# Ten of 32 modulation rows weighted on TensorE, transposed tiles emptied by two engines, first weights in three parts

## The chip, the cores and the metric

The kernel runs on one core of one Trainium2 chip. The metric is device time in microseconds of one execution of the whole program. The core's engines have instruction queues of their own and meet at semaphores: TensorE (PE, with PEld for its weight loads), VectorE (DVE), ScalarE (ACT), GpSimd (POOL) and SyncE (SP), which here mostly issues DMAs.

## The reference, cut to what matters

A transformer block over 512 tokens of width 1024: adaptive normalisation, one wide input projection, gated linear attention and dilated attention, a merge, and a convolutional FFN. The change touches its very beginning, the first modulation and the first projection:

```
mod = silu(c) @ ada_w + ada_b                  # 1024 -> 6*1024; shift1, scale1 are its first two parts
h = rmsnorm(x, norm1_w) * (1 + scale1) + shift1
... = h @ w_in                                 # av, the attention values, comes first in the kernel
```

## The kernel before, in words

Everything is kept with features on the 128 partitions. x is loaded by tokens, normalised per token on ACT, and transposed by PE into eight tiles of 128 features by 512 tokens (KT = 8; `first_tiles` makes tiles 0 to 3 into banks 3 to 6, `normed_tile(k)` tiles 4 to 7 into the same banks, so tile k waits until tile k-4 has been copied out). ACT copies all eight to xn (`normed_out`).

The modulation of a pair of feature tiles j (j = 0 to 3) needs silu(c) times eight row blocks of ada_w, each 128x512. `ada_sums` on DVE adds the weighted rows k = 0 to 7 into row 0, one scalar_tensor_tensor for each. `shift_scale(j)` on PE then sums over the partitions: a `column_sum` per 128 columns, four narrow products (32 columns of weights, one moving column of ones) each, so 16 products per row. PE may also weight a row itself, by using silu(c) in place of the ones: for j = 1 this is done for row 7 (DIRECT). For j = 0 the sums are made in two halves (`first_sums`, 256 columns each), one for feature tile 0 and one for tile 1, each with its own column sums (`first_shift_scale`) and gain (`first_shift_and_gain`). `shift_and_gain(j)` on DVE adds ada_b and makes the gain.

With gain and shift, ACT makes h_hi (`high(k)`) and the full modulated tile (`modulated(k)`), and DVE the low half h_lo (`lower(k)`); for k = 6 and 7 `modulate_late` on DVE makes the full tile. Each product of the kernel is three: high by high, low by high, high by low. Weights are split likewise: ACT writes w_hi from raw, DVE then w_lo (`early_hi`, `early_lo`, `split_hi`, `split_lo`).

The first projection runs k by k while the modulation is still being made. `first_hi(k)` multiplies h_hi by 256 columns of weights (slot 0 of raw), `wide_hi(k)` by 512 columns (slot 1 for k = 0 to 3, then vx_hi and vx_lo, which come from slot 0 anew), into banks 3 to 6, so after tiles 4 to 7 are copied out. `low_tile(k)` does the products with h_lo. PE's order is written by hand: `low_tile(2j-2)`, `shift_scale(j)`, `low_tile(2j-1)`, `quarter_hi(j)` for j = 1 to 3, then `last_lo`. After that come the dense products of all further units (`product`).

raw has two slots of 1 MB. `load(q)` on SP waits until `raw_used` is at least q-1 (L480), that is, until the split of two loads earlier is done. The first two slots are loaded by `load_early(n, part)`. Part 0 holds the rows k = 0 and 1, part 1 the rest. SP's order: ada_w for j = 0, the four early parts, ada_w for j = 1 and 2, load(2) (the second half of the wide weights, at L480), ada_w for j = 3, load(3), the spill of xn, positions and constants. SP issues in this order: a wait holds up all that is behind it. `raw_used` becomes 1 with `early_lo(0, 1)` and 2 with `early_lo(1, 1)`, both right behind the gain of j = 1 on DVE.

`keep_busy` puts transposes of the identity, which nobody reads, between PE's first steps.

Of the kernel before, what the change touches and what calls it, by code (L numbers as in the profile page):

```python
# [163 lines left out]
DIRECT = {1: KT - 1}  # L164
ADA_STEPS = [2 * KT] + [KT - (j in DIRECT) for j in range(1, KT // 2)]
FIRST_SUMS = [(0, range(0, 4)), (1, range(0, 2)), (0, range(4, 8)), (1, range(2, 3)), (1, range(3, 8))]
FIRST_AT = {step: n + 1 for n, step in enumerate((kk, k) for kk, rows in FIRST_SUMS for k in rows)}
# [3 lines left out]
def hybrid_block_kernel(nc, x, c, positions, ada_w, ada_b, norm1_w, w_in, gate_w2, gate_b, gla_norm_w,  # L171
# [3 lines left out]
    with ctx:  # L175
# [135 lines left out]
        first_ps, first_mod, first_gain = sem("first_ps"), sem("first_mod"), sem("first_gain")  # L311
# [58 lines left out]
        def early_columns(n, part):  # L370

            return (slice(0, 2 * UW * (n + 1)), slice(2 * UW * (n + 1), UE))[part]
# [57 lines left out]
        def _(sp):  # L430
# [72 lines left out]
            def load_early(n, part):  # L503

                ks = KT if n == 0 else KT // 2
                rows = (slice(0, 2), slice(2, ks))[part]
                at, width = (COL_AV, UW) if n == 0 else (COL_AV + UW, 2 * UW)
                dst = raw[:, n, :].rearrange("p (k n) -> p k n", k=ks)
                sp.dma_start(dst[:, rows, :], w_in_v[:, rows, at:at + width]).then_inc(  # L509
                    first_in[n] if part == 0 else landed[n], 16)  # L510
# [5 lines left out]
            load_first(1)  # L516
            load_first(2)
# [3 lines left out]
            sp.wait_ge(xn_sb, KT)  # L521
# [135 lines left out]
        def _(act):  # L657
# [48 lines left out]
            def high(k):  # L706

                if k == 0:
                    act.wait_ge(first_gain, 1)
                else:  # L710
                    act.wait_ge(gain_done, k // 2 + 1)
                act.wait_ge(xn_sb, k + 1)
# [32 lines left out]
            def early_hi(n, part):  # L745

                act.wait_ge(first_in[n] if part == 0 else landed[n], 16)
                cols = early_columns(n, part)
                last = act.activation(w_hi[:, n, cols], raw[:, n, cols], ACT.Copy)
                last.then_inc(first_w_hi if part == 0 else hi_done, 1)  # L750
# [384 lines left out]
        def _(dve):  # L1135
# [8 lines left out]
            def ada_sums(j, half):  # L1144
# [4 lines left out]
                for k in range(half * KT // 2, (half + 1) * KT // 2):  # L1149
                    if k == 0:  # L1150
                        dve.tensor_scalar(total, total, c_silu[:, 0:1], None, ALU.mult).then_inc(ada_step, 1)
                    elif k != DIRECT.get(j):
                        dve.wait_ge(ada_step, sum(ADA_STEPS[:j]) + k)
                        dve.scalar_tensor_tensor(total, ada_rows(j, k), c_silu[:, k:k + 1], total,  # L1154
                                                 ALU.mult, ALU.add).then_inc(ada_step, 1)

            def first_sums(part):

                kk, rows = FIRST_SUMS[part]
                dve.wait_ge(silu_done, 1)  # L1160
                for k in rows:
                    if k % (KT // 2) == 0:
                        dve.wait_ge(ada_landed[k // (KT // 2)], 32)
                    own, total = (ada_rows(0, r).rearrange("p (s k n) -> p k s n", s=2, k=2)[:, kk] for r in (k, 0))
                    if k == 0:
                        dve.tensor_scalar(total, own, c_silu[:, 0:1], None, ALU.mult).then_inc(ada_step, 1)
                    else:
                        dve.wait_ge(ada_step, FIRST_AT[kk, k - 1])
                        dve.scalar_tensor_tensor(total, own, c_silu[:, k:k + 1], total,
# [15 lines left out]
            def first_shift_and_gain(kk):  # L1185

                one = slice(kk, kk + 1)
                dve.wait_ge(first_ps if kk == 0 else mod1_ps, 1)
                dve.wait_ge(vec_sb, 1)
                dve.tensor_tensor(mod_v[:, :, one], bank[7][:, 0:4].rearrange("p (s k) -> p s k", s=2)[:, :, one],  # L1190
                                  bias_v[:, :, one], ALU.add).then_inc(first_mod if kk == 0 else mod_done, 1)
                dve.wait_ge(first_mod if kk == 0 else mod_done, 1)
                dve.scalar_tensor_tensor(gain[:, 0, one], mod_v[:, 1, one], 1.0, vecs[:, V_N1 + kk:V_N1 + kk + 1],
                                         ALU.add, ALU.mult).then_inc(first_gain if kk == 0 else gain_done, 1)

            def early_lo(n, part):

                dve.wait_ge(first_w_hi if part == 0 else hi_done, n + 1)
                cols = early_columns(n, part)
                last = dve.tensor_tensor(w_lo[:, n, cols], raw[:, n, cols], w_hi[:, n, cols].bitcast(F32), ALU.subtract)  # L1200
                last.then_inc(first_w_lo if part == 0 else raw_used, 1)
# [10 lines left out]
            def modulate_late(k):  # L1212

                dve.wait_ge(gain_done, k // 2 + 1)
                dve.wait_ge(xn_sb, k + 1)
# [292 lines left out]
            first_sums(0)  # L1508
            first_sums(1)
            first_sums(2)  # L1510
            first_sums(3)
            first_shift_and_gain(0)
            early_lo(0, 0)
            first_sums(4)
            early_lo(1, 0)
            first_shift_and_gain(1)
            for j in range(1, KT // 2):
                ada_sums(j, 0)
                lower(2 * j - 2)
                ada_sums(j, 1)  # L1520
                lower(2 * j - 1)
                shift_and_gain(j)
                if j == 1:
                    early_lo(0, 1)
                    early_lo(1, 1)
                if j == 2:
                    split_lo(2)
# [238 lines left out]
        def _(pe):  # L1766
# [29 lines left out]
            def normed_tile(k):  # L1796

                pe.wait_ge(xn_sb, k - 3)
# [567 lines left out]
```

## Time and profile before

| | us |
|---|---|
| median of 3 runs | 912.95 |
| lowest and highest run | 912.14, 913.28 |
| the profiled execution | 911.84 |
| its span | 910.1 |
| PE busy (share of the span) | 890.8 (98%) |
| DVE busy | 494.5 (54%) |
| ACT busy | 368.9 (41%) |

Times in the rows are microseconds from the span's start. A row of the timeline has start, duration, engine, line, operation, what is written from what is read, and how often; a bracket tells how long the engine idled before it and for whom. [...]

### The profile page before, as it was taken

What the parts mean: (1) busy time and instruction counts of PE and PEld (TensorE: products, weight loads), DVE (VectorE), ACT (ScalarE), POOL (GpSimd) and SP (SyncE); (2) the same over time, 40 slices, a digit from 0 to 9 for tenths busy, and PEclk for the clock granted to TensorE, in tenths of its full rate; (3) what the DMA queues carried; (4) which work ended last, traced back from release to release, by engine and by line L of the source; (5) the groups of instructions that cost most, each with busy time, mean ns of one, the idle gap of its engine ahead of it and who ended that gap; (6) DMA issues with size and microseconds to landing.
All of it is one profiled execution on the core that took longest, in us unless ns stands there. A gap on an engine that the chain in (4) does not pass through costs nothing.

```text
span 910.1 us, 12538 instructions
## 1 busy us (share of the span) xinstructions
PE 890.8 (98%) x4995; PEld 759.3 (83%) x4995; DVE 494.5 (54%) x580; ACT 368.9 (41%) x461; POOL 36.1 (4%) x33
## 2 busy tenths in 40 slices
PE   6999999999999999999999999999999999999996
PEld 5898888889898988888888888888888888888885
DVE  6878875627373656542544576555555556433333
ACT  6551226593535365332223344333333334322235
POOL 0010000000000000000021200000000000000003
PEclk9999999999999999999999999999999999999998
DMA  9976745115251525452333331333333332332202
GB/s 322 304 247 167 192 95 161 48 47 175 103 185 48 186 93 185 148 175 94 120 110 131 102 93 47 95 105 108 104 96 92 92 92 92 118 111 94 93 0 93
DMA packets 117136, 112.96 MB, mean 124 GB/s; under 512 B 7412, under 2 KB 107126, under 8 KB 114663
## 3 DMA queue, kind: packets, MB, share of 16 engines
q1 hardware_dynamic: 116375, 110.21, 38.8%
q10 hardware_dynamic: 720, 2.16, 0.7%
q8 instruction: 30, 0.49, 0.2%
q14 instruction: 11, 0.09, 0.0%
HBM read 104.80 MB, written 4.21 MB: 120 GB/s over the span
## 4 chain that ended last, share of the span: by engine, by line
PE 90%; DVE 3%; SPq 2%; DMA 2%; issue 1%; ACT 1%; DVEq 0%; ACTq 0%
PE bank L1772 26%; PE bank L1774 26%; PE bank L1773 26%; DVE ada_in L1154 1%; DMA ada_in<-in_ada_w_dram 1%; PE bank L2279 1%; PE bank L1916 1%; PE bank L1954 1%; PE bank L2044 1%; PE bank L2012 1%; PE bank L1911 1%; SPq L500 1%; PE bank L1927 1%; SPq L509 1%; PE bank L1949 1%
## 5 line engine op out<-in xcount | busy, mean ns | idle before, releaser
L1772 PE MATMUL bank<-h_hi,w_hi 128*128 128x512 f32 x672 | 264.1, 393 | 0.0
L1774 PE MATMUL bank<-h_hi,w_lo 128*128 128x512 f32 x672 | 261.6, 389 | 0.0
L1773 PE MATMUL bank<-h_lo,w_hi 128*128 128x512 f32 x672 | 261.6, 389 | 0.0
L1774 PEld LDWEIGHTS bank<-h_hi,w_lo 128*128 128x128 f32 x672 | 126.1, 188 | 26.6
L1772 PEld LDWEIGHTS bank<-h_hi,w_hi 128*128 128x128 f32 x672 | 126.2, 188 | 26.1 <-issue 0.2
L1773 PEld LDWEIGHTS bank<-h_lo,w_hi 128*128 128x128 f32 x672 | 126.2, 188 | 25.7 <-issue 0.2
L1227 DVE TENSOR_TENSOR w_lo<-raw,w_hi 128x2048 fp32r<-128x2048 f32 (+2 forms) x44 | 81.0, 1853 | 90.7 <-ACT w_hi L672 90.7
L1234 DVE TENSOR_TENSOR w_lo<-raw,w_hi 128x2048 fp32r<-128x2048 f32 x31 | 71.1, 2293 | 86.4 <-ACT w_hi L680 86.4
L1726 DVE SCALAR_TENSOR_TENSOR conv<-bank,vecs,conv 128x511 f32<-128x511 f32 x88 | 65.7, 748 | 65.8 <-ACT conv L1086 60.3
L680 ACT ACTIVATE w_hi<-raw 128x2048 fp32r<-128x2048 f32 x31 | 59.1, 1908 | 69.3 <-PE bank L1774 69.3
L672 ACT ACTIVATE w_hi<-raw 128x2048 fp32r<-128x2048 f32 (+2 forms) x42 | 67.9, 1631 | 46.9 <-DMA raw<-in_w_in_dram 34.1
L1086 ACT ACTIVATE conv<-bank,vecs 128x512 f32<-128x512 f32 x44 | 34.2, 780 | 104.6 <-PE bank L1774 104.6
L1772 PE MATMUL bank<-hs_hi,w_hi 128*128 128x512 f32 x176 | 68.6, 389 | 0.0
L1774 PE MATMUL bank<-hs_hi,w_lo 128*128 128x512 f32 x176 | 68.5, 389 | 0.0
L1773 PE MATMUL bank<-hs_lo,w_hi 128*128 128x512 f32 x176 | 68.5, 389 | 0.0
L1773 PEld LDWEIGHTS bank<-hs_lo,w_hi 128*128 128x128 f32 x176 | 33.0, 188 | 6.9
L1774 PEld LDWEIGHTS bank<-hs_hi,w_lo 128*128 128x128 f32 x176 | 33.0, 188 | 6.8
L1772 PEld LDWEIGHTS bank<-hs_hi,w_hi 128*128 128x128 f32 x176 | 33.0, 188 | 6.8
L1772 PE MATMUL bank<-w_hi,h_hi 128*128 128x256 f32 x128 | 36.5, 285 | 0.1
L1774 PE MATMUL bank<-w_hi,h_lo 128*128 128x256 f32 x128 | 36.2, 283 | 0.0
L1773 PE MATMUL bank<-w_lo,h_hi 128*128 128x256 f32 x128 | 36.2, 283 | 0.0
L1261 DVE SCALAR_TENSOR_TENSOR ada_acc<-raw,c_silu,ada_acc 128x2048 f32<-128x2048 f32 x14 | 32.9, 2347 | 0.0
(280 smaller groups left out, 1234.6 us busy)
## 6 DMA issues: line engine op xcount, KB each, us to landing
raw<-in_w_up_dram SPq DMA_DIRECT2D x44, 512.0 KB, 4.7
raw<-in_w_in_dram SPq DMA_DIRECT2D x17, 1024.0 KB, 5.3
raw<-in_ada_w_dram SPq DMA_DIRECT2D x16, 1024.0 KB, 5.5
raw<-in_w_in_dram SPq DMA_DIRECT2D x22, 512.0 KB, 5.4
raw<-in_w_down_dram SPq DMA_DIRECT2D x22, 512.0 KB, 3.7
ada_in<-in_ada_w_dram SPq DMA_DIRECT2D x16, 512.0 KB, 9.2
raw<-in_w_gla_branch_dram SPq DMA_DIRECT2D x4, 1024.0 KB, 5.0
raw<-in_w_out_dram SPq DMA_DIRECT2D x4, 1024.0 KB, 5.6
```

The source lines that it names most:

```text
L500: sp.dma_start(qk[32 * half:32 * half + 32, g, a // 2, a % 2, :], rope[32 * a:32 * a + 32, j % 2, half, :]).then_inc(qk_in[j % 2], 16)
L509: sp.dma_start(dst[:, rows, :], w_in_v[:, rows, at:at + width]).then_inc(first_in[n] if part == 0 else landed[n], 16)
L672: last = act.activation(hv, r, ACT.Copy)
L680: act.activation(w_hi[:, slot, :], raw[:, slot, :], ACT.Copy).then_inc(hi_done, 1)
L1086: act.activation(conv[:, s, t, :], bank[2 * (1 - s) + t][:, :], ACT.Identity, scale=vecs[:, bass.ds(i + (V_CW2 + t * FT), 1)], bias=vecs[: ...
L1227: last = dve.tensor_tensor(lv, r, hv.bitcast(F32), ALU.subtract)
L1234: dve.tensor_tensor(w_lo[:, slot, :], raw[:, slot, :], w_hi[:, slot, :].bitcast(F32), ALU.subtract).then_inc(raw_used, 1)
L1261: ins = dve.scalar_tensor_tensor(ada_acc[:, :], src, c_silu[:, k:k + 1], ada_acc[:, :], ALU.mult, ALU.add)
L1726: ins = dve.scalar_tensor_tensor(conv[:, s, t, tap:SEQ], src[:, 0:SEQ - tap], vecs[:, bass.ds(i + (col + t * FT), 1)], conv[:, s, t, tap:S ...
L1772: pe.matmul(out_ap, wh, xh, start=first, stop=False, skip_group_check=True)
L1773: pe.matmul(out_ap, wh, xl, start=False, stop=False, skip_group_check=True)
L1774: return pe.matmul(out_ap, wl, xh, start=False, stop=last, skip_group_check=True)
```

## The change

Four things are done together.

- PE weights rows 4 to 7 of j = 0 and j = 1 and rows 6 and 7 of j = 2 itself; none of j = 3. The half-width sums of j = 0 are gone: both feature tiles get their gain together.
- Of the eight transposed tiles, DVE copies 2, 3, 6 and 7 (`normed_copy`) and ACT 0, 1, 4 and 5. Whoever needs a tile waits for the engine that copied it (`wait_normed`).
- The 256-column weights (slot 0) are loaded and split in three parts: rows 0 and 1, rows 2 and 3, rows 4 to 7. The third is loaded behind ada_w of j = 1. `raw_used` is raised by 2 by `early_lo(0, 2)`, and no longer by part 1 of either slot.
- The orders of ACT, DVE and PE up to j = 3 are written anew; 11 of the 16 later warming transposes are gone.

```
-DIRECT = {1: KT - 1}
-ADA_STEPS = [2 * KT] + [KT - (j in DIRECT) for j in range(1, KT // 2)]
+DIRECT = (range(4, 8), range(4, 8), range(6, 8), range(0))
+ADA_STEPS = [KT - len(rows) for rows in DIRECT]
...
+            edges = ((0, 2 * UW, 4 * UW, UE), (0, 4 * UW, UE))[n]
+            return slice(edges[part], edges[part + 1])
+        def normed_by_dve(k):
+            return k % 4 >= 2
+        def wait_normed(eng, k):
+            eng.wait_ge(xn_v if normed_by_dve(k) else xn_sb, k // 4 * 2 + k % 2 + 1)
...
             load_first(0)
             for part in range(2):
                 for n in range(2):
                     load_early(n, part)
             load_first(1)
+            load_early(0, 2)
             load_first(2)
             load(2)
             load_first(3)
             load(3)
...
             early_hi(0, 0)
             high(0)
-            for k in range(2, 4):
+            high(1)
+            early_hi(1, 0)
+            for k in range(4, 6):
                 normed_out(k)
-            early_hi(1, 0)
-            for k in range(4, KT):
-                normed_out(k)
-            high(1)
             modulated(0)
             modulated(1)
             early_hi(0, 1)
             early_hi(1, 1)
             for k in (2, 3):
                 high(k)
+            early_hi(0, 2)
             for k in (2, 3):
                 modulated(k)
             split_hi(2)
...
             def early_lo(n, part):
...
+                if part < 2:
+                    last.then_inc(first_w_lo, 1)
+                else:
+                    last.then_inc(raw_used, 2)
+            def normed_copy(k):
+                dve.wait_ge(xn_ps, k + 1)
+                dve.tensor_copy(xn[:, k, :], bank[3 + k % 4][:, :]).then_inc(xn_v, 1)
...
-            first_sums(0)
...
-            first_shift_and_gain(0)
+            ada_sums(0, 0)
+            normed_copy(2)
+            shift_and_gain(0)
+            normed_copy(3)
             early_lo(0, 0)
-            first_sums(4)
+            normed_copy(6)
+            normed_copy(7)
             early_lo(1, 0)
-            first_shift_and_gain(1)
-            for j in range(1, KT // 2):
-                ada_sums(j, 0)
-                lower(2 * j - 2)
-                ada_sums(j, 1)
-                lower(2 * j - 1)
-                shift_and_gain(j)
...
+            lower(0)
+            lower(1)
+            ada_sums(1, 0)
+            early_lo(0, 1)
+            shift_and_gain(1)
+            early_lo(1, 1)
+            ada_sums(2, 0)
+            early_lo(0, 2)
+            lower(2)
+            ada_sums(2, 1)
+            lower(3)
+            shift_and_gain(2)
+            split_lo(2)
+            ada_sums(3, 0)
+            lower(4)
+            ada_sums(3, 1)
+            lower(5)
+            shift_and_gain(3)
...
             normed_tile(4)
             normed_tile(5)
-            first_shift_scale(0)
-            keep_busy(bank[0], 11)
-            first_hi(0)
+            shift_scale(0)
             normed_tile(6)
             normed_tile(7)
-            keep_busy(bank[2], 5)
-            first_shift_scale(1)
+            keep_busy(bank[0], 5)
+            first_hi(0)
+            first_hi(1)
             wide_hi(0)
-            first_hi(1)
             wide_hi(1)
```

## Rows read from the trace of the kernel before

**Rows 1.** Windows: busy us (and instructions) per engine, then granted clock, DMA share, GB/s.

```profile
22.00:62.00 40.00, 38.12 (x332) 36.09 (x332) 35.46 (x55) 18.98 (x26) 3.40 (x3) 1.00 1.00 319
62.00:910.00 848.00, 838.33 (x4555) 710.30 (x4553) 445.59 (x498) 336.61 (x415) 32.28 (x25) 1.00 0.35 110
```

**Rows 2.** Waits between 22 and 62: total us, times, longest.

```profile
ACT vx_hi L672 <- DMA raw<-in_w_in_dram: 5.0, 1, 5.0
```

**Rows 3.** Waits of SP's own queue, 0 to 62.

```profile
SPq L480 <- DVE w_lo L1200: 6.8, 1, 6.8
```

**Rows 4.** Timeline of the first stage, 17 to 52.

```profile
17.73 0.25 PEld L1807 LDWEIGHTS bank<-ones,ada_in 128*32 128x32 f32 x16 [0.22 <-issue]
...
18.52 0.82 ACT L713 ACTIVATE h_hi<-xn,mod,gain 128x512 fp32r<-128x512 f32 x1 [0.96 <-DVE gain L1193]
...
25.21 0.49 DVE L1151 TENSOR_SCALAR ada_in<-ada_in,c_silu 128x512 f32<-128x512 f32 x1 [2.17 <-DMA ada_in<-in_ada_w_dram]
...
28.71 0.53 PEld L2092 LDWEIGHTS bank<-w_hi,h_lo 128*128 128x128 f32 x4 [1.26 <-DVE h_lo L1210]
...
30.43 0.35 PEld L1807 LDWEIGHTS bank<-c_silu,ada_in 128*32 128x32 f32 x32 [0.24 <-issue]
30.43 0.43 PE L1807 MATMUL bank<-c_silu,ada_in 128*32 128x1 f32 x32
...
31.54 0.16 DVE L1179 TENSOR_TENSOR mod<-bank,vecs 128x4 f32<-128x4 f32 x1
...
31.82 2.89 DVE L1200 TENSOR_TENSOR w_lo<-raw,w_hi 128x1536 fp32r<-128x1536 f32 x2
...
33.59 0.37 SPq L480 DMA_DIRECT2D raw<-in_w_in_dram  x1
...
39.86 1.92 ACT L672 ACTIVATE vx_hi<-raw 128x2048 fp32r<-128x2048 f32 x1 [4.98 <-DMA raw<-in_w_in_dram]
...
42.01 2.29 DVE L1227 TENSOR_TENSOR vx_lo<-raw,vx_hi 128x2048 fp32r<-128x2048 f32 x1
...
43.15 0.66 PEld L2084 LDWEIGHTS bank<-w_hi,h_hi 128*128 128x128 f32 x4
...
48.93 0.66 PEld L2092 LDWEIGHTS bank<-w_hi,h_lo 128*128 128x128 f32 x4
...
50.60 0.69 DVE L1210 TENSOR_TENSOR h_lo<-n_first,h_hi 128x512 fp32r<-128x512 f32 x1
...
51.34 0.53 PEld L2092 LDWEIGHTS bank<-w_hi,h_lo 128*128 128x128 f32 x4 [0.16 <-DVE h_lo L1210]
```

**Rows 5.** DMAs issued at 33.59, 21.43, 34.55: us to landing; then all of this size.

```profile
raw<-in_w_in_dram SPq DMA_DIRECT2D x1, 1024.0 KB, 6.2
...
ada_in<-in_ada_w_dram SPq DMA_DIRECT2D x1, 512.0 KB, 9.7
...
ada_in<-in_ada_w_dram SPq DMA_DIRECT2D x1, 512.0 KB, 8.3
...
raw<-in_w_in_dram SPq DMA_DIRECT2D x17, 1024.0 KB, 5.3
```

**Rows 6.** Groups by form, 0 to 62: busy us, mean ns of one, idle before.

```profile
L1154 DVE SCALAR_TENSOR_TENSOR ada_in<-ada_in,c_silu 128x512 f32<-128x512 f32 x20 | 15.0, 751 | 0.6
...
L713 ACT ACTIVATE h_hi<-xn,mod,gain 128x512 fp32r<-128x512 f32 x8 | 6.2, 816 | 12.3 <-DVE gain L1182 11.3 <-DVE gain L1193 1.0
...
L743 ACT ACTIVATE xn<-bank 128x512 f32<-128x512 f32 x8 | 4.2, 598 | 0.4 <-PE bank L1791 0.4
...
L1200 DVE TENSOR_TENSOR w_lo<-raw,w_hi 128x1536 fp32r<-128x1536 f32 x1 | 1.8, 1750 | 0.0
...
L1151 DVE TENSOR_SCALAR ada_in<-ada_in,c_silu 128x512 f32<-128x512 f32 x3 | 1.4, 483 | 2.2 <-DMA ada_in<-in_ada_w_dram 2.2
```

**Rows 7.** Groups by form, DVE, whole span: a 128x512 copy out of a bank.

```profile
L1366 DVE COPY PT<-bank 128x512 f32<-128x512 f32 x8 | 5.1, 686 | 7.0 <-PE bank L1927 7.0
```

**Rows 8.** Windows at the end, columns as in rows 1.

```profile
903.50:904.00 0.50, 0.00 (x0) 0.00 (x0) 0.50 (x2) 0.50 (x2) 0.00 (x0) 0.63 0.63 238
```

More of the change, by code:

```diff
@@ L505, in load_early @@
                 ks = KT if n == 0 else KT // 2
-                rows = (slice(0, 2), slice(2, ks))[part]
+                rows = (slice(0, 2), slice(2, 4), slice(4, ks))[part]
                 at, width = (COL_AV, UW) if n == 0 else (COL_AV + UW, 2 * UW)
@@ L509, in load_early @@
                 sp.dma_start(dst[:, rows, :], w_in_v[:, rows, at:at + width]).then_inc(
-                    first_in[n] if part == 0 else landed[n], 16)
+                    (first_in[n], landed[1] if n == 1 else mid_in, landed[0])[part], 16)
             load_first(0)
@@ L1151, in ada_sums @@
                         dve.tensor_scalar(total, total, c_silu[:, 0:1], None, ALU.mult).then_inc(ada_step, 1)
-                    elif k != DIRECT.get(j):
+                    elif k not in DIRECT[j]:
                         dve.wait_ge(ada_step, sum(ADA_STEPS[:j]) + k)
                         dve.scalar_tensor_tensor(total, ada_rows(j, k), c_silu[:, k:k + 1], total,
[L1155 to L1169, printed above, removed]
                                                  ALU.mult, ALU.add).then_inc(ada_step, 1)
@@ L1183, in shift_and_gain @@
                                          ALU.add, ALU.mult).then_inc(gain_done, 1)
[L1185 to L1194, printed above, removed]
             def early_lo(n, part):
-                dve.wait_ge(first_w_hi if part == 0 else hi_done, n + 1)
+                if part < 2:
+                    dve.wait_ge(first_w_hi, 2 * part + n + 1)
+                else:
+                    dve.wait_ge(hi_done, 2)
                 cols = early_columns(n, part)
                 last = dve.tensor_tensor(w_lo[:, n, cols], raw[:, n, cols], w_hi[:, n, cols].bitcast(F32), ALU.subtract)
-                last.then_inc(first_w_lo if part == 0 else raw_used, 1)
+                if part < 2:
+                    last.then_inc(first_w_lo, 1)
+                else:
+                    last.then_inc(raw_used, 2)
+            def normed_copy(k):
+                dve.wait_ge(xn_ps, k + 1)
+                dve.tensor_copy(xn[:, k, :], bank[3 + k % 4][:, :]).then_inc(xn_v, 1)
             def lower(k):
@@ L1811, in shift_scale @@
             def shift_scale(j):
[L1813 to L1816 removed]
+                direct = list(DIRECT[j])
+                for n_row, row in enumerate(direct + [0]):
+                    if n_row == 0:
                         pe.wait_ge(silu_done, 1)
+                        pe.wait_ge(ones_set, 1)
                         pe.wait_ge(ada_landed[2 * j + 1], 32)
[L1819 to L1821 removed]
+                        if j > 0:
+                            pe.wait_ge(mod_done, j)
+                    if row == 0:
                         pe.wait_ge(ada_step, sum(ADA_STEPS[:j + 1]))
                     for n in range(4):
[L1824 to L1825 removed]
+                        last = column_sum(bank[7], 4 * j + n, ada_rows(j, row)[:, n * P:(n + 1) * P],
+                                          ones[:, 0:1] if row == 0 else c_silu[:, row:row + 1],
+                                          n_row == 0 and n == 0, row == 0)
                 last.then_inc(mod1_ps, 1)
[L1828 to L1836 removed]
             def take(i):
```

57 lines of the change are left out of this document (14 added, 43 removed).

## The prediction

> **What bounds the kernel now.** I read the windows first: PE is busy 838.3 of the 848 us after 62 us [rows 1]. So the products after 62 are PE's alone, and whatever moves their start moves the end by as much. The change lies before that, where DVE is busy 35.5 of the 40 us from 22 to 62 and PE 38.1. Then the waits of that stretch: ACT stands 5.0 us for one transfer, the second half of the wide weights [rows 2]. The queue's waits name the third party: SP stands 6.8 us at its load of that transfer (L480) until DVE has written a w_lo [rows 3]. The timeline then gives the times [rows 4]. One chain runs through DVE: weighted rows of ada_w in steps of four, a lower() between them, the column sums on PE, the gain. It starts at 25.21, when the rows for j=1 land, and ends at 51.34, where PE has waited for the h_lo written from 50.60. From there PE idles no more than tenths of a microsecond before the dense products. So 51.34 is the mark: what moves it moves the end.
>
> One thing in these rows decides my forecast. The wide transfer is issued at 33.59, when DVE's early_lo(0,1) ends (the pair starts at 31.82, and 1750 ns for its 1536 columns [rows 6] end at 33.57). It lands 6.2 us later, at 39.8 [rows 5]; ACT, which waited for it, makes vx_hi from 39.86 to 41.78; DVE starts vx_lo at 42.01. There are only 0.2 us of slack between this transfer and DVE's chain.
>
> **The change, part by part.**
>
> *First modulation (j=0).* DVE loses the half-width sums and keeps four full rows; PE weights rows 4 to 7 itself. PE's column sum of a row is 16 products, 32 records, ending 0.43 us after its start; eight products load in 0.25 and sixteen in 0.35 [rows 4]. One further row costs between 0.20 (twice that difference) and 0.43 (all of it again). I take 0.27, nearer the low end, as they follow each other without a wait. Five rows: 0.43 + 4 x 0.27 = 1.5. They start where the present ones do, 17.73, after tile 5, since the rows landed before. Now high(0) starts at 18.52, 0.8 after eight products that end within 0.3; with 1.5 in place of 0.3 DVE adds at 19.3 and ACT starts high(0) at 19.7. But this now holds the gain of k=0 and 1, which ACT used to get late.
>
> *Copies of the transposed tiles.* Four of eight go from ACT (598 ns) to DVE (686 ns in the nearest row, other 128x512 copies out of a bank) [rows 6, 7]. The third stands before the gain in DVE's idle time and is free. The fourth stands behind the gain: 19.7 to 20.4. PE's tile 7 needs that bank, so tile 7 and five warming products (0.5 and 0.6) end at 21.5. first_hi(0) starts there, against 19.39 before, and 16 products of 256 columns and 16 of 512 take 5.8 us, as the same set does from 43.15 to 48.93 [rows 4]: 27.3. ACT's own line (two high at 816 ns, a 1024-column w_hi at 1.0, half of vx_hi's 1.92, two copies) ends at 23.6, where wide_hi(0) stands anyway. low_tile(0), which started at 28.71 after an idle 1.26, starts at 27.3: this part gains about 1.4 on PE.
>
> *DVE to j=1.* lower(0) and lower(1) now stand before the sums of j=1. ACT's modulated(0) and (1), the same instruction as high, are done by 25.2, the second lower (0.69) by 25.9. Four rows are 483 + 3 x 751 ns = 2.7: 28.6, against a start at 25.21 before. The move of 512 KB of first weights behind those rows brings them in some 1.6 us earlier (0.52 MB at the 319 GB/s of [rows 1]), which is worth nothing, as DVE is not free before 25.9.
>
> *shift_scale(1).* low_tile(0) to the column sums is 1.7 (28.71 to 30.43): 29.0. Four direct rows and the sum, 1.5, as all five are ready: 30.5. DVE adds at 30.6 instead of 31.54, a gain of 0.9. Three weighted rows of DVE (2.3 us) have gone, but PE pays 0.8 of it, and PE is on this path.
>
> *The release of raw.* Before, DVE wrote early_lo(0,1) at once and so freed slot 0. Now neither slot is freed until early_lo(0,2), which stands behind early_lo(1,1) and behind the whole sums of j=2: 30.6 + 0.3 + 1.2 + 2.7 + 1.2 = 36.0, where 0.3 is the 31.54 to 31.82 of before and 1.2 a 1024-column w_lo (2.89 for the pair less 1.75, and a little). SP's load(2) waits for that, and queued behind it on SP are the four transfers of ada_w for j=3, load(3), the spill of xn, positions and constants. So the wide transfer goes out at 36.0, not 33.59: **2.4 us late**. It can't be much better: the sums of j=2 can't begin before their rows land, 21.43 + 9.7 = 31.1 [rows 5], and 31.1 + 2.7 + 1.2 = 35.0 is still 1.4 late. The worst is both modulations with 0.43 a row, 0.64 later each: 3.7 late.
>
> *What that does.* It lands at 42.2; vx_hi is done at 44.1 and DVE starts vx_lo at 44.2, 2.2 after 42.01. ACT's high(4) stands behind vx_hi in its order, so PE stands from some 41.9 to 45.0. From 44.2 DVE's chain is the old one (two halves of j=3, not weighted by PE at all): the lower of 50.60 comes at 52.8 and PE's 51.34 becomes 53.5. PE itself would be ready at 45.0 + 5.8 + 1.4 (a low_tile: the 1.7 less the 0.3 before its column sums) = 52.2, before DVE's sums at 52.9, so PE's stall costs nothing beyond that. The rows of j=3 have room: their first half landed at 34.55 + 8.3 = 42.9, lands at 45.3, and is wanted at 46.4.
>
> *j=2.* Rows 6 and 7 go to PE: 1.5 us off DVE, 0.5 on PE. Both run in the time in which DVE and ACT wait for the wide transfer, so I cost them at nothing and they bring nothing; if that cover were gone, they would bring about 1.0.
>
> **The sum.** Release 2.4 late, less 0.2 of old slack: +2.2. Everything behind is PE's and shifts. The profiled execution is 911.84 (span 910.1), so 914.0 by its own time; the median of the runs stands 1.1 above it, so the forecast is 912.95 + 2.2 = **915.2**.
>
> **The rivals.**
>
> *The clock falls.* From 17.7 to 21.5 PE gets narrow products, two tiles and a wait, with 11 warming products fewer, and later it stands some 3 us at 41.9. The trace shows the clock falling when PE thins out: after its last, broken-up products the granted clock averaged 0.63 between 903.5 and 904.0 [rows 8]. [...] Against it: PE has idled for 1.3 us at 28 at full clock. [...]
>
> *The late transfer is no bound (not slower).* Place: SP's load(2) at L480. If the transfer still landed by 39.9, PE's gain stays: low_tile(1), the same 5.8, low_tile(2) and three rows end at 30.5 + 1.4 + 5.8 + 1.7 + 1.0 = 40.4, the gain follows 0.4 later, and vx_lo starts at 40.8 instead of 42.01: -1.2, 911.8. It decides from a release at 33.8 or before. For it speaks only that other 1 MB loads of w_in took 5.3 us in the median [rows 5], which is not enough; against it stands the floor of 35.0 above.
>
> *The transfer is quicker.* It meets empty queues. With 5.3 in place of 6.2 it is +1.3: 914.2. Before, it met nearly empty queues too, with 6.2.
>
> **How the numbers follow.** A measurement tells about 0.2% from no change, 1.8 us here. Forecast, release late and clock full: 0.68, spread +1.3 to +3.5 by the bounds. Clock: 0.12. Quick transfer: 0.12. No bound: 0.08. Range: from the quick transfer at its best (+0.4) to the upper bound and the start of the clock's case (+3.9): 913.3 to 916.9, leaving out the last rival and most of the clock's. Slower by over 0.2%: 0.12 and some 0.7 of 0.68, 0.60. Faster: the part of the last rival where PE's gain is more than I have, and what I have overlooked, 0.06. Within: 0.34.
>
> **What would show it.** Right: SP's load(2) near 36.0 with DVE's 1024-column w_lo just before; ACT waiting for it until about 42.2; vx_lo near 44.2; a PE stall of some 3 us for h_hi at 42 to 45; low_tile(5) near 53.5; low_tile(0) near 27.3 and the add of j=1 near 30.6. Wrong: load(2) before 34.5, DVE idle less than 1 us before vx_lo, a PE stall elsewhere, or a granted clock under 1 before 62 us.

## The result and the profile after

The changed kernel takes 918.88 us (median of 6 runs, 917.64 to 919.16), the kernel before 912.13 (6 runs, 911.48 to 913.28): 1.007 times as long, between 1.0057 and 1.0083. That is **6.4 us slower** (5.2 to 7.6), with the sign of the forecast and about three times its size. 918.88 lies outside the range of 913.3 to 916.9. The profiled execution took 918.54 us. The page of its profile:

```profile
span 916.8 us, 13073 instructions
PE 893.2 (97%) x5272; PEld 761.5 (83%) x5272; DVE 489.9 (53%) x566; ACT 366.8 (40%) x458; POOL 36.1 (4%) x33
```

DVE did lose work (489.9 against 494.5 us) and ACT 2.1 us, and the span grew by 6.7. So I read the windows of the changed kernel first, to find where it grew (length, then PE, PEld, DVE, ACT and POOL busy, the granted clock, the DMA share, GB/s).

```profile
16.00:20.00 4.00, 2.31 (x167) 2.01 (x166) 0.01 (x1) 0.77 (x2) 0.00 (x0) 1.00 1.08 367
20.00:22.00 2.00, 0.00 (x0) 0.00 (x0) 0.00 (x0) 0.00 (x0) 0.00 (x0) 0.82 1.09 350
22.00:28.00 6.00, 4.81 (x22) 4.32 (x22) 4.09 (x8) 4.22 (x7) 0.00 (x0) 0.50 1.10 350
68.00:917.00 849.00, 839.41 (x4559) 711.29 (x4558) 446.99 (x500) 337.46 (x416) 32.28 (x25) 1.00 0.36 110
```

The last row answers to [rows 1]: behind 68 us PE is as full as it was behind 62. The loss is all ahead of it. The second row shows something that no window of before between 14 and 30 has: for two whole microseconds PE, DVE and ACT all do nothing. Behind it the granted clock is 0.50 for six. The timeline of that place:

```profile
16.82 1.14 PEld L1806 LDWEIGHTS bank<-c_silu,ada_in 128*32 128x32 f32 x127 [0.17 <-issue]
17.91 0.41 PE L1806 MATMUL bank<-ones,ada_in 128*32 128x1 f32 x29
23.19 0.16 PE L1806 MATMUL bank<-ones,ada_in 128*32 128x1 f32 x1 [4.87 <-issue]
23.39 0.16 DVE L1172 TENSOR_TENSOR mod<-bank,vecs 128x4 f32<-128x4 f32 x1 [7.38 <-PE bank L1806]
23.78 1.52 ACT L719 ACTIVATE h_hi<-xn,mod,gain 128x512 fp32r<-128x512 f32 x2 [7.01 <-DVE gain L1175]
```

The five rows of narrow products for j = 0 run from 16.82 to 18.32. (A record is one instruction as the trace lists it. Each of the 80 narrow products shows as two matmul records, each of the 16 transposes of tiles 4 to 7, float32 too, as one.) There only one of their 160 matmul records is still to come, and PE stands for **4.87 us before it**. Nothing that the profile shows holds it: "issue". DVE waits 7.38 for the sum and ACT 7.01 for the gain behind it. In the view of waits from 16 to 62 the stop has a row of its own, with no engine and no DMA as its releaser:

```profile
PE bank L1806 <- issue: 4.9, 1, 4.9
```

The marks that the prediction named, in the timeline of the changed kernel:

```profile
32.71 0.65 PEld L2082 LDWEIGHTS bank<-w_hi,h_lo 128*128 128x128 f32 x4
36.13 0.16 DVE L1172 TENSOR_TENSOR mod<-bank,vecs 128x4 f32<-128x4 f32 x1 [3.42 <-PE bank L1806]
41.54 0.37 SPq L487 DMA_DIRECT2D raw<-in_w_in_dram  x1
46.67 1.91 ACT L681 ACTIVATE vx_hi<-raw 128x2048 fp32r<-128x2048 f32 x1 [6.26 <-DMA raw<-in_w_in_dram]
48.61 2.29 DVE L1220 TENSOR_TENSOR vx_lo<-raw,vx_hi 128x2048 fp32r<-128x2048 f32 x1 [2.19 <-ACT vx_hi L681]
49.33 0.53 PEld L2074 LDWEIGHTS bank<-w_hi,h_hi 128*128 128x128 f32 x4 [1.92 <-ACT h_hi L719]
57.94 0.53 PEld L2082 LDWEIGHTS bank<-w_hi,h_lo 128*128 128x128 f32 x4 [0.16 <-DVE h_lo L1203]
65.79 0.35 PE L2158 MATMUL bank<-cst,rows_b 88*128 88x88 f32 x2 [0.26 <-DMA rows_b<-in_conv_b_dram]
68.72 0.19 PEld L1771 LDWEIGHTS bank<-h_hi,w_hi 128*128 128x128 f32 x1
```

The row of SPq is SP issuing load(2), in 0.37 us. The last row is the first weight load of the dense products. Its counterpart in the timeline of before:

```profile
61.66 0.19 PEld L1772 LDWEIGHTS bank<-h_hi,w_hi 128*128 128x128 f32 x1
```

So the dense products begin 7.06 us later, and the forecast had them 2.2 later, at 63.86.

### The profile page after: what moved, and what is told of

The parts are those of the page before. It is cut to its first block, busy times and chain, and to the rows that moved or that the text cites. A ratio compares the mean times of both kernels' runs of the same rounds, so it can differ in the third digit from the quotient of the medians.

```text
span 916.8 us, 13073 instructions
## 1 busy us (share of the span) xinstructions
PE 893.2 (97%) x5272; PEld 761.5 (83%) x5272; DVE 489.9 (53%) x566; ACT 366.8 (40%) x458; POOL 36.1 (4%) x33
## 4 chain that ended last, share of the span: by engine, by line
PE 92%; SPq 2%; DVE 2%; DMA 2%; ACT 1%; issue 1%; DVEq 0%; ACTq 0%
PE bank L1771 27%; PE bank L1773 26%; PE bank L1772 26%; PE bank L2267 1%; DMA rows_b<-in_conv_b_dram 1%; PE bank L1906 1%; PE bank L1944 1%; PE bank L2034 1%; PE bank L2002 1%; PE bank L1901 1%; PE bank L1917 1%; PE bank L1806 1%; PE bank L1939 1%; PE bank L2044 1%; PE bank L2023 1%
```

## The experiments

The theory after this reading (A): PE ran out of **instructions**. Instructions are brought in by blocks, the narrow products are used up faster than the next block comes, and the idle time lets the clock fall. Nothing read up to here shows that; it was an assumption. The rivals: (B) the products themselves, or their operands, are slow at that place; (C) the late release of raw explains all that is lost; (D) the clock alone does. Each kernel was timed beside runs of the kernel before on the same chip (911.49 for the four e, 911.95 for the four f, 911.32 for the three g). Kernels of different groups are compared by their ratios to before, which is 1.0070 for the changed kernel. Edits are against the changed kernel if nothing else is said.

### e1_wide: the same sums with a quarter of the instructions

```
+            def wide_sum(dst, at, weights, moving, first, last):
+                return pe.matmul(dst[:, at:at + 1], weights, moving, start=first, stop=last, skip_group_check=True)
...
-                        last = column_sum(bank[7], 4 * j + n, ...
+                        last = wide_sum(bank[7], 4 * j + n, ...
```

> The changed kernel with one edit: each column sum of 128 columns in the first four modulation steps is one product with 128 columns of weights instead of four with 32, the same arithmetic with a quarter of PE's instructions (20 products in place of 80 at j=0). Theory A (PE runs out of instructions: its 80 narrow products are 320 instructions in about 1.5 us, and the packet with the next ones comes behind the full DMA rings): the 4.9 us in which PE waits for nothing visible before its last narrow product vanish, the granted clock stays 1.00 from 20 to 28, and PE's column sums of j=0 take 1.5 to 2.6 us. The kernel is then 4 to 5 us faster than the changed one and still 1.5 to 3 us slower than the one before, because the second wide transfer is still released late (load near 36 to 38). Theory B (PE waits for data: the landing of the weighted rows, or the accumulation of rows into one bank): the stall stays at 4 to 5 us whatever the shape, and the time stays within 1 us of the changed kernel's.

It took 924.14 us, 1.0139 [1.0122, 1.0155]. The stop is gone, as A has it; but the time grew by some 6 us over the changed kernel where a gain of 4 to 5 was expected. The timeline of this kernel:

```profile
16.75 4.61 PE L1812 MATMUL bank<-c_silu,ada_in 128*128 128x1 f32 x32
21.22 1.84 PE L1812 MATMUL bank<-ones,ada_in 128*128 128x1 f32 x8
```

And its windows, columns as above:

```profile
18.00:19.00 1.00, 1.00 (x11) 1.00 (x11) 0.00 (x0) 0.00 (x0) 0.00 (x0) 1.00 1.06 365
18.00:20.00 2.00, 2.00 (x17) 2.00 (x16) 0.00 (x0) 0.00 (x0) 0.00 (x0) 0.80 1.08 358
20.00:22.00 2.00, 2.00 (x11) 2.00 (x10) 0.00 (x0) 0.00 (x0) 0.00 (x0) 0.50 1.12 352
```

40 records with 128 columns of weights take 6.3 us where 160 with 32 columns took 1.5: 0.09 us each at a granted clock of 1.00 (11 in 1.00) and 0.18 at 0.50 (11 in 2.00), against 9 ns. And the clock fell to 0.50 although PE shows as busy for the whole of the window. The edit also widens the sums of j = 1, which take 5.9 us from 33.37 in place of 1.5, so load(2) goes out at 44.70, later still. The run speaks for A on the stop, and settles nothing on the time.

### e2_dve_first: DVE weights all rows of j = 0

```
-DIRECT = (range(4, 8), range(4, 8), range(6, 8), range(0))
+DIRECT = (range(0), range(4, 8), range(6, 8), range(0))
...
             normed_copy(2)
+            ada_sums(0, 1)
             shift_and_gain(0)
```

> The changed kernel with no row of j=0 weighted by PE: DVE adds all eight rows (3.1 us more on DVE, behind its copy of tile 2), PE does only the 16 narrow products with ones. Theory A (instructions): no stall at j=0, none at j=1 or 2 either, though PE still has 80 narrow products in a row at j=1, because there it has the next block of instructions already; the gain of j=0 comes 1.1 us later than it would without stall, the second wide transfer goes out near 37, and the time is 1.5 to 3.5 us above the kernel before, 3 to 5 below the changed one. Theory B (rows weighted on PE wait for data or for the bank): no stall at j=0 either, but one of several microseconds at j=1, where as many rows are weighted while the transfers are in full flow, and then the time is within 2 us of the changed kernel's.

914.57 us, 1.0033 [1.0022, 1.0043]: by the two ratios some 3.4 us come back with 64 products taken out (128 matmul records and as many loads), although DVE now works longer before the first gain. There is no stop at j = 0, nor at j = 1, whose products run straight through; its window from 30 to 32:

```profile
30.00:32.00 2.00, 2.00 (x143) 1.75 (x145) 0.00 (x0) 0.00 (x0) 0.00 (x0) 1.00 1.07 337
```

B falls: the same five rows of products, with the same kind of operands, are not slow at j = 1. C falls as the whole cause, as the release is still behind early_lo(0, 2). Not all is back: load(2) goes out at 37.83.

### e3_pad: the kernel before, with 64 more narrow products

```
             first_shift_scale(0)
-            keep_busy(bank[0], 11)
+            for row in range(4):
+                for n in range(4):
+                    column_sum(bank[0], n, ident, ones[:, 0:1], True, True)
```

(Against the kernel before; nobody reads these products.)

> The kernel before, with 64 narrow products whose sums nobody reads (identity by ones, into a bank that is free then) in place of the 11 warming transposes behind the first column sums: 1.1 us of PE against 1.4, no data that is late, no accumulation, no other edit. Theory A (instructions): PE stops for 3 to 5 us within some 2 us after them, at an instruction that waits for nothing visible, until the packet of the instruction queue has come, and the granted clock may fall; the time grows by 1 to 5 us, as DVE's chain behind the column sums of the second tile has some slack. Theory B (waits for data or accumulation of weighted rows): no stall and a time within 0.5 us of the kernel before.

914.78 us, 1.0031 [1.0018, 1.0043]. Nothing of the change is in this kernel but more narrow products (in place of 11 warming transposes), and it has a stop, shorter than the 3 to 5 us expected, on another instruction, the last transpose of a tile whose first ones have run. Its timeline:

```profile
18.32 1.24 PE L1807 MATMUL bank<-ones,cst 128*32 128x1 f32 x127
24.84 0.48 PE L1800 MATMUL bank<-cst,x_tok 128*128 128x128 f32 x1 [2.34 <-issue]
```

Then I counted records, by the window of this kernel from the start of the program up to the stop (first row):

```profile
0.00:24.70 24.70, 13.59 (x222) 11.80 (x222) 14.28 (x29) 14.07 (x23) 0.41 (x5) 0.92 0.98 326
21.00:22.00 1.00, 1.00 (x7) 1.00 (x6) 0.94 (x3) 1.00 (x2) 0.00 (x0) 0.50 1.10 348
```

The second row belongs to the clock: it is at 0.50 from 21 to 22, with PE shown as busy, before PE stops at 22.5.

In the changed kernel the window up to its stop has the same count (the first row is for the table below):

```profile
0.00:17.11 17.11, 10.21 (x98) 8.88 (x101) 8.37 (x14) 9.94 (x16) 0.42 (x5) 1.00 0.93 313
0.00:23.10 23.10, 11.41 (x222) 10.02 (x223) 8.37 (x14) 9.94 (x16) 0.42 (x5) 0.96 0.97 325
```

222 matmuls and 222 or 223 loads, in two kernels whose instructions before it differ. That is a place in the stream of instructions, not in the work.

### e4_release: e2, and raw released early

```
             early_hi(1, 1)
+            early_hi(0, 2)
             for k in (2, 3):
                 high(k)
-            early_hi(0, 2)
...
             early_lo(0, 1)
+            early_lo(0, 2)
             shift_and_gain(1)
             early_lo(1, 1)
             ada_sums(2, 0)
-            early_lo(0, 2)
...
-                if part < 2:
-                    last.then_inc(first_w_lo, 1)
-                else:
-                    last.then_inc(raw_used, 2)
+                last.then_inc(raw_used if part == 2 or (n, part) == (1, 1) else first_w_lo, 1)
...
-                    if k < 4:
+                    if 2 <= k < 4 and part == 1:
+                        pe.wait_ge(raw_used, 2)
+                    elif k < 4:
```

(And e2's edit.)

> The kernel of the run without PE-weighted rows at j=0, with one more edit: the third part of the 256-column weights is split on ACT right behind part 1 of the wide ones and on DVE ahead of the gain of j=1, and raw_used rises with it and with part 1 of the wide weights singly, so that the load of the second wide half goes out near 30.5 instead of 37. If the late release is what is left of the loss (my forecast's mechanism): the wide transfer lands before 37, ACT and DVE do not wait for it, PE has no stall for h_hi near 42 to 45, and the time falls by 2 to 3 us against that run, to within 1 us of the kernel before. Rival (the release is hidden, and the loss is PE's extra products and the later gain of j=0): the time falls by less than 0.7 us.

912.05 us, 1.0003 [0.9993, 1.0013]; one execution of 2308.95 us, unlike all others, is left out. It is 2.5 under e2. The chain is the one of the forecast, run backwards: load(2) at 30.55, 7.3 us earlier than in e2, and ACT's wait for it down from 6.5 to 1.8. The timeline of e4_release:

```profile
30.55 0.37 SPq L487 DMA_DIRECT2D raw<-in_w_in_dram  x1
36.94 1.92 ACT L681 ACTIVATE vx_hi<-raw 128x2048 fp32r<-128x2048 f32 x1 [1.76 <-DMA raw<-in_w_in_dram]
```

The granted clock is still 0.50 in the window from 20 to 22, just behind a wait of PE of 2.3 us for DVE's sum of j = 0.

### f1_fewer: the stop moved by 36 instructions

```
-            keep_busy(bank[0], 18)
             first_tiles()
```

> The changed kernel without the 18 warming transposes that PE does first: 36 instructions fewer ahead of the same 80 narrow products of j=0, nothing else. Theory A (PE executes its instructions faster than the next block comes, so it stops at a fixed count of instructions): the stop no longer falls on the last narrow product but some 36 instructions later, behind the column sums, among the warming transposes or first products behind tile 7, and it is shorter by what PE waits there anyway: 0 to 3 us in place of 4.9. The gain of j=0 comes near 19.5 in place of 23.6, and the time falls by 1 to 4 us against the changed kernel, less if the granted clock falls early because the warming is gone. Theory B (the stop belongs to that product, or to the rows weighted): the last narrow product still starts 4 to 5 us after its neighbours.

917.84 us, 1.0068 [1.0053, 1.0084], which can't be told from the changed kernel's 1.0070: the gain of 1 to 4 us that was expected is missed. The 18 transposes (a load and a matmul each: 25 of both in the first stage, where the changed kernel has 43) that are missing move the stop behind the column sums, which now end at 19.1, into first_hi(0), by the timeline of f1_fewer:

```profile
24.28 1.22 PE L2074 MATMUL bank<-w_lo,h_hi 128*128 128x256 f32 x4 [1.55 <-issue]
```

The window up to it:

```profile
0.00:24.20 24.20, 11.53 (x222) 10.40 (x222) 12.87 (x22) 14.52 (x23) 0.41 (x5) 0.93 0.97 325
```

Again 222, and a third kind of instruction. (The trace puts the idle time of the weight load beside it down to a w_lo of DVE; the one that it needs had ended at 20.70.) The gain of j = 0 came over four microseconds earlier than in the changed kernel, and at the end next to nothing was left of it. Between the two lie a shorter stop and the lower clock, which is 0.50 from 21, more than a microsecond before this stop; their shares were not measured apart.

### f2_warm: e4 with 16 warming transposes before the column sums of j = 0

```
             normed_tile(5)
+            keep_busy(bank[0], 16)
             shift_scale(0)
```

> The kernel with early release and no PE-weighted rows at j=0, with 16 warming transposes ahead of the column sums of j=0, where PE now idles 2.3 us for DVE's sums: 32 instructions and 2.1 us of PE in that idle time. There the granted clock fell to 0.50 between 20 and 23. If that fall costs what the rows at the lower level show (products of 256 columns at twice their time): the clock stays 1.00 and the time falls by 0.5 to 1.3 us against that kernel. Rival (the fall is hidden, since PE waits for ACT's copies and for w_hi there anyway): no more than 0.3 us.

912.78 us, 1.001 [1.0001, 1.0019]. The clock is 1.00 all through 14 to 28, and the kernel is no faster than e4 (1.0003): missed. What is new is in its waits between 16 and 62, and in its timeline:

```profile
PE bank L2111 <- issue: 0.9, 1, 0.9
43.06 1.44 PE L2111 MATMUL bank<-w_hi,h_lo 128*128 128x512 f32 x3 [0.93 <-issue]
```

Behind the 48 products of j = 2, after 473 matmul records, there is a small stop, which e4 has not: the warmers are instructions too. The granted clock is 0.50 from 43 to 46 behind it. A stop of 0.29 stands at 34.43, after 346 records. So this run does not price the clock, as more than one thing changed in it. D falls by the changed kernel's own windows: its granted clock is 1.00 from 16 to 20, when the stop has begun.

### f3_two: rows 6 and 7 of j = 0 to PE, the rest as e4

```
-DIRECT = (range(0), range(4, 8), range(6, 8), range(0))
+DIRECT = (range(6, 8), range(4, 8), range(6, 8), range(0))
...
-            shift_and_gain(2)
             split_lo(2)
+            shift_and_gain(2)
...
             normed_tile(6)
+            keep_busy(bank[0], 6)
             normed_tile(7)
-            keep_busy(bank[0], 5)
+            keep_busy(bank[0], 2)
```

(Against e4.)

> Early release as before, but PE weights two rows of j=0 (6 and 7) in place of none or four, so 48 narrow products in place of 80; six and two warming transposes around tile 7; and DVE writes vx_lo before the gain of j=2, where it idled 3 us for PE. Theory A (instructions): 192 instructions do not use up the blocks at hand, no stall. The gain of j=0 comes near 19.4, column sums of j=1 end near 30.4, DVE's chain is no longer last at j=3, PE is: 1 to 2.2 us faster than the kernel before, 910 to 911 where that is 911.5. Theory B (rows weighted by PE wait for data): a stall of microseconds at j=0 or j=1, and slower than the kernel before.

915.46 us, 1.0043 [1.0029, 1.0057]: some 3.5 worse than e4, with nothing wrong at j = 0 (the add at 18.61, no stop). The expectation from A is missed, and a stop at j = 1 is what had been written down for B. It has come back at j = 1, in the timeline of f3_two:

```profile
28.97 0.19 PE L1804 MATMUL bank<-ones,ada_in 128*32 128x1 f32 x3
34.04 0.59 PE L1804 MATMUL bank<-ones,ada_in 128*32 128x1 f32 x27 [4.88 <-issue]
```

And the windows that end before and at it:

```profile
0.00:27.95 27.95, 19.84 (x222) 18.09 (x226) 18.33 (x30) 16.19 (x25) 0.41 (x5) 1.00 0.99 328
0.00:34.00 34.00, 21.05 (x348) 19.21 (x348) 19.55 (x31) 17.25 (x26) 0.41 (x5) 0.95 1.00 329
```

348 is 222 + 126, and 126 matmuls with their loads are 252 records. Against B stands that j = 1 has the same 80 products as in e2 and e4, where they run through: what differs is where they lie in the stream. The count speaks for A: this kernel passes its 222nd matmul without a stop and has one 126 further on, as with blocks of one length, and whether PE stops at the end of one depends, by A, on when the block before was used up.

### f4_warm_vx: f2, and vx_lo before the gain of j = 2

```
-            shift_and_gain(2)
             split_lo(2)
+            shift_and_gain(2)
```

(Against f2.)

> The kernel with early release and warming, no PE-weighted rows at j=0, and vx_lo on DVE before the gain of j=2: if DVE's chain is what is last at j=3 (its wait of 3 us at the gain of j=2 is then used), 0.5 to 1.2 us faster than the same without this exchange; if PE is last there, no difference above 0.2 us.

914.03 us, 1.0019 [1.001, 1.0028], with runs from 911.76 to 915.22. The gain of 0.5 to 1.2 us over f2 (1.0010) did not come, and why is **inconclusive**. The profiled execution is the fastest one, and has no stop. A stop that comes in some executions and not in others would make such a spread, but no trace of a longer one was taken; that is only argued.

### g1_best: two direct rows for each j, and raw released early

```
-DIRECT = (range(4, 8), range(4, 8), range(6, 8), range(0))
+DIRECT = (range(6, 8), range(6, 8), range(6, 8), range(0))
...
             normed_copy(2)
+            ada_sums(0, 1)
             shift_and_gain(0)
...
             ada_sums(1, 0)
+            ada_sums(1, 1)
             early_lo(0, 1)
             shift_and_gain(1)
+            early_lo(0, 2)
             early_lo(1, 1)
             ada_sums(2, 0)
-            early_lo(0, 2)
```

(And e4's edits of early_hi, raw_used and PE's wait, f3's order of split_lo(2) and its warmers.)

> What the runs so far point to: PE weights two rows (6 and 7) of each of j=0, 1 and 2, so at most 48 narrow products (192 instructions) stand in a row; raw_used rises early (the third part of the 256-column weights is split right behind the gain of j=1, before the wide part 1); six and two warming transposes around tile 7; vx_lo behind the gain of j=2, as in the changed kernel. Theory A (a fixed block of instructions, refilled some 6 us after it is asked for while the rings are full): no stop of PE at 222 or 348 products, granted clock 1.00 from 16 to 60; column sums of j=1 end near 29.5 to 30.5, of j=2 near 39 to 40, and the low products that began at 51.34 in the kernel before begin at 48.5 to 50. Time 1.3 to 2.8 us below the kernel before. If rows weighted by PE were the trouble, whatever their number, it would be slower than the kernel before.

**909.83 us, 0.9982 [0.9973, 0.9991]: faster than both kernels**, by 1.6 us against before and by some 8 against the changed one. The three rows of j = 0 (96 records) go through between 17.88 and 19.00, PE waits for "issue" only once behind them, 0.41 at 43.23, and the clock is full over the whole stretch, by its window:

```profile
14.00:62.00 48.00, 47.01 (x567) 44.27 (x566) 41.24 (x68) 25.46 (x35) 3.23 (x3) 1.00 1.02 327
```

The timeline of g1_best:

```profile
31.56 0.37 SPq L487 DMA_DIRECT2D raw<-in_w_in_dram  x1
49.92 0.53 PEld L2081 LDWEIGHTS bank<-w_hi,h_lo 128*128 128x128 f32 x4
60.24 0.19 PEld L1770 LDWEIGHTS bank<-h_hi,w_hi 128*128 128x128 f32 x1
```

The second row is the mark low_tile(5), at 51.34 before and at 57.94 after.

### g2_two_late: the same direct rows, late release as in the change

```
-DIRECT = (range(4, 8), range(4, 8), range(6, 8), range(0))
+DIRECT = (range(6, 8), range(6, 8), range(6, 8), range(0))
...
             normed_copy(2)
+            ada_sums(0, 1)
             shift_and_gain(0)
...
             ada_sums(1, 0)
+            ada_sums(1, 1)
             early_lo(0, 1)
```

> The changed kernel with its own orders, its one late rise of raw_used and its warming, but rows 6 and 7 in place of 4 to 7 weighted by PE at j=0 and j=1 (DVE adds rows 4 and 5 there). This is the forecast's mechanism without the stop: no stop of PE; load of the second wide half at 35 to 36.5, ACT waiting for it until about 41, DVE's vx_lo near 43, PE waiting 1 to 3 us for h_hi there. Time 0 to 2 us above the kernel before, 5 to 7 below the changed one, and 2 to 3.5 above the kernel with early release of this call.

912.02 us, 1.0004 [0.9995, 1.0013]. This is the forecast's own mechanism without the stop, in the timeline of g2_two_late:

```profile
36.16 0.37 SPq L487 DMA_DIRECT2D raw<-in_w_in_dram  x1
41.24 1.91 ACT L681 ACTIVATE vx_hi<-raw 128x2048 fp32r<-128x2048 f32 x1 [7.18 <-DMA raw<-in_w_in_dram]
43.18 2.29 DVE L1220 TENSOR_TENSOR vx_lo<-raw,vx_hi 128x2048 fp32r<-128x2048 f32 x1 [3.08 <-ACT vx_hi L681]
43.91 0.74 PE L2076 MATMUL bank<-w_hi,h_hi 128*128 128x256 f32 x4 [2.50 <-ACT h_hi L719]
```

load(2) goes out at 36.16 (forecast of the change: 36.0), and PE stands 2.50 for h_hi at 43.9 (forecast: some 3). It is 2.2 slower than g1 (which has its order of split_lo(2) and its warmers beside the release; e4 against e2, with the release alone, gave 2.5) and, by the two ratios to before (1.0070 and 1.0004), 6.0 faster than the changed kernel. So the late release costs about **2.2 to 2.5**, and the further rows on PE, with the stop and the clock, about **6**.

### g3_drained: the changed kernel with its queues empty at the stop

```
                     load_early(n, part)
+            sp.wait_ge(mod1_ps, 1)
             load_first(1)
```

> The changed kernel with one wait more on SP: the transfers for j=1 and all behind them are issued only after the column sums of j=0, so that the rings have all but drained when PE's next instructions are asked for; 80 narrow products in a row as in the changed kernel. Theory A with full rings as the cause of the long refill: PE still stops at product 222, since the number of instructions is the same, but for 0.5 to 3 us in place of 4.9. If the refill takes as long whatever the transfers do, 4 to 5 us stay. The time as a whole rises by several microseconds in both cases, as all transfers behind come later.

917.04 us, 1.0056 [1.0038, 1.0075] (two runs), so no longer than the changed kernel, where several microseconds more were expected. SP issues no further transfer until the column sums of j = 0 are done. The stop stays on the same record and shrinks by more than half, in the timeline of g3_drained:

```profile
20.98 0.16 PE L1807 MATMUL bank<-ones,ada_in 128*32 128x1 f32 x1 [2.10 <-issue]
```

Its window from 18 to 20, and the row of one queue in its DMA view from 18.5 to 19.0:

```profile
18.00:20.00 2.00, 0.88 (x106) 0.81 (x96) 0.00 (x0) 0.00 (x0) 0.00 (x0) 0.99 0.32 116
q8 instruction: 1, 0.02, 11.5%
```

The share of the DMA engines between 18 and 20 is 0.32 at 116 GB/s, where the changed kernel has 1.08. So what PE waits for comes sooner when the data's transfers are out of the way.

**Together.** In every kernel with a stop I took the time from the end of one block earlier, by A some 126 matmuls before it (about the 96th matmul for a stop at the 222nd, then the 222nd and the 348th) to the record behind the stop. The profile's DMA views have a queue named "instruction" (q8), and between the second and the fourth column of each row there is one packet of it, of 0.02 MB; I take it for the block that comes in. The third column is the tenth of a microsecond in which that packet is recorded.

| kernel | a block earlier | packet | PE goes on | between |
|---|---|---|---|---|
| changed | 17.11 | 20.7 | 23.19 | 6.1 |
| f1_fewer | 18.01 | 21.7 | 24.28 | 6.3 |
| e3_pad | 18.44 | 22.2 | 24.84 | 6.4 |
| f3_two (222 to 348) | 27.95 | 31.4 | 34.04 | 6.1 |
| f2_warm (222 to 346) | 29.7 | 32.0 | 34.43 | 4.7 |
| f2_warm (348 to 473) | 34.6 | 40.4 | 43.06 | 8.5 |
| g1_best (348 to 473) | 36.40 | 40.6 | 43.23 | 6.8 |
| g3_drained | 17.68 | 18.6 | 20.98 | 3.3 |

From the packet to PE's going on it is 2.3 to 2.7 us in every row, with the queues full or empty. What varies is the time before the packet: 2.3 to 5.8 while the transfers run at 330 to 362 GB/s, and 0.9 in g3. For the same crossing, the 222nd, it is 3.6 to 3.8 in the first three rows, and the 2.7 that g3 saves on the changed kernel's 3.6 is what its stop is shorter by (2.10 against 4.87). No run tells what makes it 2.3 at one crossing and 5.8 at another. Kernels that use a block more slowly do not stop there: before takes 11.2 from its 96th to its 223rd matmul, and g1 8.0 from 28.41 to its 348th. The windows of the kernel before:

```profile
0.00:20.10 20.10, 12.45 (x96) 11.15 (x97) 11.60 (x25) 11.46 (x19) 0.41 (x5) 1.00 0.95 317
0.00:31.31 31.31, 22.54 (x223) 20.19 (x223) 20.35 (x40) 18.99 (x29) 0.41 (x5) 1.00 1.00 329
```

The packet of the changed kernel, in its DMA view between 20.5 and 21.0:

```profile
q8 instruction: 1, 0.02, 14.1%
```

So what the runs show of the blocks is the counts (222, 346 to 348 and 473, some 126 apart) and one packet of the queue ahead of each stop. When a block is asked for, and how many instructions are held ahead, no run shows. One crossing cost 4.87 us: behind these narrow products it was not hidden.

## Why the prediction was wrong

Step by step, on PE's path to the dense products, the forecast against the changed kernel's timeline:

| step | forecast | measured | adds |
|---|---|---|---|
| column sums of j = 0 start | 17.73 | 16.82 | -0.9 |
| from there to high(0) | 1.97 | 6.96 | +5.0 |
| high(0) to low_tile(0) | 7.6 | 8.93 | +1.3 |
| low_tile(0) to the add of j = 1 | 3.3 | 3.42 | +0.1 |
| add to load(2) | 5.4 | 5.41 | 0 |
| load(2) to vx_hi | 6.2 | 5.13 | -1.1 |
| vx_hi to low_tile(5) | 11.3 | 11.27 | 0 |
| low_tile(5) to the dense products | 10.3 | 10.78 | +0.5 |

The sum is +4.9, the whole way from 63.86 to 68.72. The first step may be no more than scatter: with the same work of PE ahead of it, this start is 17.41 in f3, 17.62 in g2 and 17.88 in g1. The forecast's base, 912.95 from three runs, was itself 0.8 above the median of the six.

**The failed step** is "*First modulation (j=0)*", in its sentence "Five rows: 0.43 + 4 x 0.27 = 1.5". The products do take that, 16.82 to 18.32 without the last one, and 1.5 again at j = 1. But I priced 160 matmul records and as many loads, of some 9 ns each (1.5 us for 160), by their duration alone, as if the next instruction were always there. What the step costs is 1.5 plus a stop of 4.87. That mechanism stands nowhere among my rivals.

**The clock.** The rival had the right place. The forecast's range takes in the start of its case (+3.9), a term that no run shows; measured are 1.3 at most, the excess of the step from high(0) to low_tile(0), which has a granted clock of 0.50 from 23 to 28. In the changed kernel the clock fell inside the stop, at 21 to 22 (0.65 there, 1.00 before), so it did not cause it. Whether the stop caused the fall is not shown: in e3 and f1 the clock was at 0.50 before their stops began, and in e1 it fell without one, each time behind many one-column products. Most of the loss is the stop, which the rival has not. No run here prices the clock by itself.

**The late release** was right, in mechanism and size. The wait at L487 is the longest of SP's, its load(2) is issued 5.41 after the add of j = 1 as forecast, DVE idles 2.19 before vx_lo, and PE stalls for h_hi (its weight load 1.92 in place of 3, as PE was itself late). g1 and g2 put it at 2.2, with the order of vx_lo and the warmers changed beside it, and e2 and e4, with the release alone, at 2.5; the forecast was +2.2. (The lower end of its spread, +1.3, is +1.2 by its own working, 1.4 less 0.2.)

**The transfer** took 5.1 us and not 6.2: the third rival, and the value of the other 1 MB loads [rows 5]. I chose the one row of the same transfer over the median of its kind, and the median was right, also in g2 (36.16 to 41.24). In e4, where it goes out among other transfers (348 GB/s before it), it took 6.4.

**The end**: the half microsecond behind low_tile(5) was counted at nothing. 0.26 of it is a wait for rows_b, which is loaded behind load(2) in SP's order; my list of what is queued behind SP's wait ended before it.

**What DVE gained**, 4.6 us less busy time, can't be seen in the changed kernel's time.

## What to carry to other kernels

Cost many tiny matmuls by number as well as by duration: in this kernel some 250 PE instructions that were used up before the next block had come, 4.7 to 8.5 us after the block before while the DMA queues were full, ran into a stop of up to 4.9 us. An idle time marked "issue" in the middle of like instructions (4.87 us here) is the sign; count the records up to it, and look at whether another kernel stops at the same count. A few rows moved to another engine and an early release of a buffer were worth 1.6 us here, where many rows and a late release lost 6.4.

## What was not expected of the hardware

- Where PE stopped for "issue" between 16 and 62 us, it was at the same counts of its instructions, whatever these were: matmul 222 in four kernels, 346 to 348 in two, 473 in two. PE went on 2.3 to 2.7 us after a packet of the instruction queue, with full and with drained queues; the packet itself came 2.3 to 5.8 us after the block before was used up with full queues, and 0.9 with drained ones.
- Matmuls of float32 with one moving column cost 9 ns a record with 32 columns of weights (1.5 us for 160), and 90 ns with 128 at a granted clock of 1.00, 180 at 0.50 (e1_wide). Four narrow ones (8 records, some 75 ns) are less than half as dear as one wide one (2 records, 180 ns at 1.00).
- In e1_wide the granted clock fell to 0.50 with PE shown as busy throughout, and in e3_pad it was 0.50 from 21 to 22 before the stop. In both, the busy share of one-column products did not tell whether they keep the clock.
